# Turning x without its root: two transformer stacks on one core

## What is computed

```python
# first block, per layer
x = x + 0.5 * swiglu(rmsnorm(x, ffn1_norm), ffn1_w_in, ffn1_w_out)       # D_FF = 2816
x = x + hybrid_mixer(rmsnorm(x, mix_norm), w_in, ...)   # delta rule, stick-breaking attention, gates
x = x + 0.5 * swiglu(rmsnorm(x, ffn2_norm), ffn2_w_in, ffn2_w_out)
# second block, per layer
x = x + hybrid_mixer_2(rms_norm(x, mix_norm), ...)      # two attentions, gated mixing, w_out
x = x + memory_cross_attention(rms_norm(x, mem_x_norm), mem, ...)        # h @ mem_w_q, softmax, @ mem_w_o
x = x + conv_gated_ffn(rms_norm(x, ffn_norm), w_up, conv_w, conv_b, w_down)
# at the end
return rms_norm(x, final_norm)
# with
rmsnorm(x, g) = x * rsqrt(mean(x * x, over a row) + 1e-6) * g
swiglu(h, w_in, w_out) = (silu(h @ gate) * (h @ up)) @ w_out             # gate, up = halves of w_in
```

## Time and profile before

| | us |
|---|---|
| median of 3 runs | 2601.81 |
| lowest, highest | 2601.13, 2605.77 |
| profiled execution | 2607.15 |
| its span in the trace | 2605.3 |
| TensorE busy | 2448.4 (94%) |
| GpSimd busy | 1790.0 (69%) |
| ScalarE busy | 1115.8 (43%) |
| VectorE busy | 948.4 (36%) |

### The profile page before, as it was taken

One profiled execution on the slowest core, in us unless ns is written; L12 is line 12 of the kernel. 1 busy time (PEld: TensorE's weight loads), 2 busy tenths in 40 slices (PEclk: granted clock), 3 DMA queues, 4 the chain that ended last, 5 costly groups with the idle time before them and its releaser, 6 DMA issues.

```text
span 2605.3 us, 45928 instructions
## 1 busy us (share of the span) xinstructions
PE 2448.4 (94%) x17692; PEld 2292.1 (88%) x17692; DVE 948.4 (36%) x1554; ACT 1115.8 (43%) x1248; POOL 1790.0 (69%) x1372
## 2 busy tenths in 40 slices
PE   7999999998899999999999889999888999898998
PEld 7999888988899899888889889999788998787997
DVE  1114555322311211245543241112424564423564
ACT  4334434445333433444343634335454335454333
POOL 6998444455799789864445667996545997544996
PEclk9999999998999999999999899999899999899999
DMA  6554332323455455442233334564233555323553
GB/s 207 191 179 150 109 97 87 109 90 105 131 192 179 162 180 191 146 150 94 82 98 106 106 129 152 187 203 129 82 98 114 189 182 164 105 72 107 170 185 121
DMA packets 312052, 360.11 MB, mean 138 GB/s; under 512 B 18604, under 2 KB 290912, under 8 KB 311776
## 3 DMA queue, kind: packets, MB, share of 16 engines
q1 hardware_dynamic: 311904, 358.08, 42.4%
HBM read 357.00 MB, written 1.05 MB: 137 GB/s over the span
## 4 chain that ended last, share of the span: by engine, by line
POOL 43%; issue 26%; PE 25%; DVE 3%; ACT 2%; POOLq 0%; DVEq 0%; ACTq 0%
POOL sb_lo L458 43%; PE ps L482 21%; PE ps L911 1%; PE ps L887 1%; PE ps L799 1%; ACT sb_kT L1002 0%; ACT sb_sq L1328 0%; PE ps L524 0%; DVE sb_negmax L1802 0%; PE ps L960 0%; POOLq L453 0%; ACT sb_levels L1301 0%; PE ps L894 0%; DVE sb_kT L1745 0%; PE ps L869 0%
## 5 line engine op out<-in xcount | busy, mean ns | idle before, releaser
L458 POOL TENSOR_TENSOR sb_lo<-sb_raw,sb_hi 128x512 fp32r<-128x512 f32 x1368 | 1789.8, 1341 | 794.0 <-ACT sb_hi L991 791.8
L482 PE MATMUL ps<-sb_hT_h,sb_hi 128*128 128x256 f32 x3524 | 1026.6, 291 | 33.3 <-DVE sb_hT_l L1434 10.6
L482 PE MATMUL ps<-sb_hT_h,sb_lo 128*128 128x256 f32 x3524 | 1007.0, 286 | 0.0
L482 PE MATMUL ps<-sb_hT_l,sb_hi 128*128 128x256 f32 x3524 | 1006.6, 286 | 0.0
L991 ACT ACTIVATE sb_hi<-sb_raw 128x2048 fp32r<-128x2048 f32 x342 | 655.3, 1916 | 797.1 <-PE ps L482 792.3
L482 PEld LDWEIGHTS ps<-sb_hT_h,sb_hi 128*128 128x128 f32 x3524 | 684.5, 194 | 50.3 <-issue 31.3
L482 PEld LDWEIGHTS ps<-sb_hT_h,sb_lo 128*128 128x128 f32 x3524 | 685.3, 194 | 3.6 <-issue 1.4
L482 PEld LDWEIGHTS ps<-sb_hT_l,sb_hi 128*128 128x128 f32 x3524 | 684.6, 194 | 0.0
L482 PE MATMUL ps<-sb_hi,sb_o_h 128*128 128x512 f32 (+1 forms) x720 | 265.4, 369 | 9.9 <-DVE sb_o_l L1441 9.9
L482 PE MATMUL ps<-sb_hi,sb_o_l 128*128 128x512 f32 (+1 forms) x720 | 263.4, 366 | 0.0
L482 PE MATMUL ps<-sb_lo,sb_o_h 128*128 128x512 f32 (+1 forms) x720 | 262.7, 365 | 0.0
(11 more groups left out here) (320 smaller groups left out, 2811.0 us busy)
## 6 DMA issues: line engine op xcount, KB each, us to landing
sb_raw<-in_ffn_w_in SPq DMA_DIRECT2D x88, 1024.0 KB, 5.1
sb_raw<-in_w_in SPq DMA_DIRECT2D x78, 1024.0 KB, 5.2
sb_raw<-in_ffn_w_out SPq DMA_DIRECT2D x44, 1024.0 KB, 5.0
sb_raw<-in_ffn_w_up SPq DMA_DIRECT2D x44, 1024.0 KB, 5.1
sb_raw<-in_ffn_w_down SPq DMA_DIRECT2D x22, 1024.0 KB, 4.8
sb_raw<-in_w_out SPq DMA_DIRECT2D x16, 1024.0 KB, 5.1
sb_raw<-in_w_branch_a SPq DMA_DIRECT2D x8, 1024.0 KB, 5.1
sb_raw<-in_w_branch_b SPq DMA_DIRECT2D x8, 1024.0 KB, 5.1
```

The costliest lines, as they stand in the source:

```text
L458: ins = nc.gpsimd.tensor_tensor(lo[:, slot, c], raw[:, slot, c], hi[:, slot, c].bitcast(F32), ALU.subtract)
L482: ins = mm(dst, s, m, start=first and n == 0, stop=last and n == 3 * len(pairs) - 1)
```

## The change

1. **Networks, the memory's queries.** x is turned as it is (`turn`), without the root. The gain is applied as before in the high and low parts. The inverse root of each row is made meanwhile (`squares`, `diagonal`), put on the diagonal of a 128 x 256 tile, and one matmul with ones (`turn_row`) spreads it over all partitions; ScalarE copies it to `row` (`take_row`). VectorE multiplies the outputs by it in PSUM (`by_row`): gate and up of every chunk, and the memory's queries, which ScalarE no longer copies. Silu waits for `gate_scaled`. Mixers keep the old entry. The filler transposes ahead of the changed entries go.
2. **x comes in pieces.** Additions to x are in four pieces (strips of 256 columns after mixers, 512 columns of one row tile after networks and memory), each releasing `x_ready`. Groups of two block rows are turned as soon as their columns are there: three groups after mixers while the last units run, two groups inside the last unit after a network (only between layers of the first block) or memory.
3. **The first two units interleave** (`enter`): a part of the gate's block rows, the late transposes, the same part of the up unit, the row's matmul, the rest of the gate, the rest of up. On ScalarE the splits of the third and fourth unit stand before Silu of the first chunk as before, but between them the row is copied.
4. **Loads.** x in two tiles, the identity and ones come first, the rest of the constants after the first five units; the nine vectors of layer 0 go out on ScalarE's queue, those of layer 1 during the second network of layer 0. The first unit is split by quarters, on ScalarE and VectorE. The loop over the layers of the first block is written out.

```diff
+            def turn(g, bank):
+                for i in range(2):
+                    for t in range(ST):
+                        k = 2 * g + i
+                        ins = nc.tensor.transpose(ps[:, bank, i * S + t * P:i * S + (t + 1) * P], x[:, t, k * P:(k + 1) * P], ident)
+                ins.then_inc(tr_ready, 1)
+            def turn_row(e, bank):
+                pe.wait_ge(diag_ready, e + 1)
+                ins = mm(ps[:, bank, 0:S], cc("ones"), diag, start=True, stop=True)
+                ins.then_inc(row_turned, 1)
+            def enter(e, n, q, b, units, banks, row_bank, early, landed=True):
+                (u0, bank0), (u1, bank1) = units
+                split_at = 2 * early
+                feature_part(b, u0, bank0, q, 0, split_at, landed)
+                if early < 4:
+                    pe.wait_ge(x_ready, updates(n))
+                    for g in range(early, 4):
+                        turn(g, banks[g])
+                    feature_part(b, u1, bank1, q, 0, split_at)
+                    turn_row(e, row_bank)
+                    feature_part(b, u0, bank0, q, split_at, KB)
+                    feature_part(b, u1, bank1, q, split_at, KB)
+                else:
+                    turn_row(e, row_bank)
+                    feature_part(b, u1, bank1, q, 0, KB)
...
-                transposes(3 * l + 2)
-                ffn(2 * l + 1, b + (FFN_UNITS + MIX1_UNITS) // RING, 3 * l + 2, sil_ready, 2 * NCH * l + NCH)
+                enter(2 * l + 1, 3 * l + 2, 3 * l + 2, b2, ((0, AFTER_MIX_GATE), (1, 1)), TURN_BANKS, ROW_BANK, 3)
+                if l + 1 < DEPTH:
+                    columns(16 * V1_LOADS * (l + 2), 1, 2)
+                ffn(2 * l + 1, b2, sil_ready, 2 * NCH * l + NCH, 3 * l + 3 if l + 1 < DEPTH else None)
...
+            def enter(e, n, q, gain, banks, row_bank, early, next_split):
+                squares(n)
+                for g in range(early, 4):
+                    high_pair(q, g, gain, hT_h, banks[g])
+                diagonal()
+                next_split(0)
+                take_row(e, row_bank)
+                next_split(1)
...
+                def silu(j, bank=0):
+                    act.wait_ge(gate_scaled, F0 + j + 1)
+                    fn(sil[:], ps[:, bank, :], ACT.Silu).then_inc(sil_ready, 1)
-                split(b, 2)
-                split(b, 3)
-                silu(b, 0, None)
+                silu(0, bank_of_first)
...
-                def chunk(bb, ku, kd, j, parts=act_parts):
+                def chunk(bb, kg, ku, kd, j, parts=act_parts, bank=0):
+                    dve.wait_ge(unit_done, RING * bb + (kg + RING + 1))
+                    by_row(ps[:, bank, :], ps[:, bank, :]).then_inc(gate_scaled, 1)
                     dve.wait_ge(act_ready, F0 + j + 1)
+                    dve.wait_ge(unit_done, RING * bb + (ku + RING + 1))
+                    own.link(by_row(ps[:, 1, :], ps[:, 1, :]))
                     dve.wait_ge(sil_ready, F0 + j + 1)
-                    dve.wait_ge(unit_done, RING * bb + (ku + RING + 1))
                     tt(prod[:], sil[:], ps[:, 1, :], ALU.mult).then_inc(up_used, 1)
```

More of the change, by code:

```diff
@@ L199 @@
 WARM = 20
+PIECES = 4
 DELTA_WEIGHT = [2, 3, 2] + [1] * 10 + [1.3, 1, 1, 1, 1, 1, 1, 1.5, 2]
@@ L272, in build_program @@
         rstd = sb("rstd", [P, 8])
+        row = sb("row", [P, S])
         negmax = sb("negmax", [P, 2, 4])
@@ L373, in ffn @@
                 gate(0, 0), up(1, 0), gate(2, 1), up(3, 1), down(4, 0)
+                if between is not None:
+                    between()
                 with sp.Fori(1, NCH - 1) as j:
@@ new lines, in squares, with diagonal @@
+            def squares(n):
+                act.wait_ge(x_ready, updates(n))
+                for t in range(ST):
+                    ins = fn(junk[:, t, :], x[:, t, :], ACT.Square, accum_out=ss[:, t:t + 1])
+                own.link(ins)
+            def diagonal():
+                own.link(rsqrt(rstd[:, 0:ST], ss[:, 0:ST], 1.0 / D))
+                for t in range(ST):
+                    ins = fn(diag[:, t * P:(t + 1) * P], ident, ACT.Copy, scale=rstd[:, t:t + 1])
+                ins.then_inc(diag_ready, 1)
@@ L1400, in _ @@
                 mixer2(l, b)
-                high(q + 2, gain2(V2_ON), hT_h)
-                for r in range(13, 17):
+                high(q + 2, gain2(V2_ON), o_h)
+                for r in range(13, 15):
                     two_next(b, r)
@@ L1808, in memory @@
                 sig = lambda ins: ins.then_inc(me_dve, 1)
-                scaled(x, n)
-                low(q + 3, gain2(V2_MEMX), hT_h, hT_l)
+                low_pair(q + 3, 3, gain2(V2_MEMX), hT_h, hT_l, MEMORY_BANKS[3])
+                dve.wait_ge(row_ready, 2 * l + (2 * DEPTH + 1))
+                for m in range(2):
+                    dve.wait_ge(unit_done, RING * b + (17 + m + RING + 1))
+                    two = lambda v: v.rearrange("p (k n) -> p k n", n=S)
+                    sig(tt(qT[:, 2 * m:2 * m + 2, :], two(ps[:, 6 + m, :]), over(row[:], 2), ALU.mult))
                 for beta in range(ME_BATCHES):
```

449 lines of the change are left out of this document (284 added, 165 removed).

## The result

| kernel | us, median (lowest to highest, runs) | before, same chip | ratio, 95% interval |
|---|---|---|---|
| changed | 2572.16 (2570.52 to 2574.12, 4) | 2602.29 | 0.9879, 0.9867 to 0.9891 |
| changed, second time | 2571.30 (2569.56 to 2575.33, 4) | 2605.73 | 0.9875, 0.9860 to 0.9891 |

The change saves 30.1 us by the first pair of medians and 34.4 by the second. Predicted were 37.7, and 2564; the range 2550 to 2586 holds the time. By the two profiled executions it is 2607.15 - 2571.15 = 36.0, span 2569.2.

A forecast was written before the change was run, and what follows sets the result against it. TensorE is busy 94% of the span, idle between stages. Savings 4.2 + 7.1 + 9.4 + 9.9 + 8.8 + 1.3 - 3 = 37.7 take the profiled 2607.15 to 2569.5; the median, 5.3 lower, gives 2564, range 2550 to 2586.

The forecast's parts named there:

- the entries' chains: Step-by-step times at stage entries; mixer to network was to take 16.8 us against 18.9, saving 4.2 for two.
- The wait that it named: Entry from mixer to network: TensorE idle from 13.3 to 15.9 us until Silu has read the gate, about 2.6 us.
- The wait of 1.1 in three entries: Entries behind a network or memory: TensorE waits 1.1 us for the second transposed group's low part, behind VectorE's last addition.
- inside the networks: Turns of a network: two products by the row a chunk, 0.69 us each on VectorE, cost nothing under TensorE's 16.98.
- rival 3: Network turns: products by the row slow GpSimd until it bounds, 19.1 us a turn, 2694; chance 0.05 with other slowness.
- The price of the rival: Network turns: GpSimd becoming the bound decides from 1.2 us of added GpSimd time a turn.
- the clock: TensorE at half rate after idle stretches: 3 us charged for seven inner entries, bounds 0 to 17.
- Rival 1: Entries: unfilled gaps keep TensorE cold (17 us) and unfound waits add 8; about 15 saved, 2587; chance 0.20.
- the memory: Two entries from mixer to memory: scores start at 14.9 us against 19.6, saving 4.7 each, 9.4 for two.
- the start: Kernel start: x, identity and first unit load earlier, first two units done at 30.4 us against 39.2; 8.8 saved.
- the ends: Ends of five networks: last addition 512 wide, 0.69 us instead of 1.22; 1.3 saved for five, bounds 0 and 2.6.
- the right column of the table: Predicted savings by stretch of the whole kernel, without the 3 us charged for half rate; sum 40.7 us.

The follow-up runs named there:

- filler in the gaps: Changed kernel with 20 identity transposes on TensorE in each gap behind a mixer and 9 behind a network, first block; 2568.36 us (0.9859).
- the orders mended: Changed kernel, first block: Silu before unit 3's split, unit 2's split right behind the squares, vectors' copy behind chunk 0; 2568.56 us (0.9850).
- orders and PSUM: Changed kernel with the orders mended and VectorE's product of Silu and up written to PSUM in all six networks; 2566.44 us (0.9863).
- the version to beat both: Changed kernel: product in PSUM, unit 2's split behind squares, Silu first only behind a network, no wait for Silu behind a mixer; 2563.86 us (0.9844).

## Why the prediction was right or wrong

*Where it was right: the entries' chains.* Behind a mixer, counted from the last product (691.6), the prediction had low parts at 2.5, 36 matmuls at 5.4, the up unit's first part at 10.2, both units at 13.3 and Silu at 15.9. The trace has 2.4, 5.4, 10.2, 13.5 and 16.1. The wait that it named, split of unit 3, table load and Silu ahead of the next gate, is there: 2.70 and 2.82 us for 2.6. A second limit stands close behind it, unseen: VectorE's copy of the next vectors, which waits for TensorE's last transposes, is in front of the product by the row at 705.38, and with the split out of the way the gap there fell only to 2.10. The wait of 1.1 in three entries was 0.8 and twice 1.14. The table load again took 1.28 us, and Silu began right behind it (705.82, 707.12); the 2.7 us that the Trainium skill's page "ScalarE: Activation LUTs", section Terms, gives for it are not seen here.

*Right: inside the networks.* The products cost nothing there (16.98 a turn; the kernel without them is no faster in the four networks of the first block), and rival 3 fell by its own condition: one SBUF input, 699 ns in the mean of 132. The price of the rival was sound too: 1.3 us a turn is free. By the page "SBUF — State Buffer" of the Trainium skill, section "Who interferes with whom", an instruction with two SBUF inputs contends with GpSimd and one with at most one doesn't, outside the modes that use both ports, which a cast can enter. The prediction left that exception out. The traces agree with both halves: the same subtraction takes 1578 ns with two SBUF inputs and 691 with one, and the cast, with its one input in SBUF, does wait.

*Right in size: the clock.* 3 us were charged for the seven inner entries, near the low end of 0 to 17, without a row that gave the number. In both traces of the changed kernel two of the seven are at half rate, the ones behind a mixer; half of 3.11 and 3.13 us of work is an estimate of 3.1, and filler in the gaps brings 2.8 back. Rival 1 had this mechanism, and overpriced it. That the charge came out is a guess that held.

*Mis-sized: the memory, the start and the ends.* Against the right column of the table, the two stages of the memory are 1.9 us short. Of this 1.4 is one small instruction of the softmax, on a 128x4 tile: VectorE's L2003 takes 0.86 us beside GpSimd's subtractions, 0.17 before, where GpSimd had paused.
```profile
1962.35 0.17 DVE L1803 TENSOR_SCALAR sb_negmax<-sb_negmax 128x4 f32<-128x4 f32 x1
```
```profile
1939.57 0.86 DVE L2003 TENSOR_SCALAR sb_negmax<-sb_negmax 128x4 f32<-128x4 f32 x1
```
In the traces with the orders mended, with orders and PSUM, and of the version to beat both it takes under 0.2, and the memory's stages are 41.1 to 41.2 us instead of 41.8: GpSimd's place in time had changed, a term that the sum didn't have. From memory to network 2.4 us are missing by the first pair and 3.7 by the second. About 0.5 an entry is the chain itself, and at the end of each convolved network the product by the row lengthens VectorE's last chunk, so that TensorE has a gap of 0.64 ahead of the last down unit, 0.4 of it waiting, where the sum had no term; 0.3 an entry stays open. The 1.3 between the pairs is half rate that the first trace of before has at 2405.6 and its second hasn't: the prediction had counted it as a saving of the entry. The start brought 7.7 and 7.1 for 8.8: the copy of the vectors came at 10.55, as said (10.5), but part of the first two units ran at half rate. Behind the last network 0.8 is lost where 0.3 was to come: the first row tile of x is now complete one piece before the last, not half a unit, and its squares begin 0.64 us ahead of the last addition and no longer 1.46. GpSimd's 16.4 us in the convolved network passed the 16.2 that I had set.

*The rest is no merit of the change.* The mixers were to be 2.6 us longer, by the transposes moved into them, and were 3.2 and 3.8 shorter. They were at half rate for 17.0 and 10.2 us less; half of that, 8.5 and 5.1, is by estimate the most that this can have given back, so it covers the 5.8 by which the first pair passes its sum and not all of the 6.4 of the second. Why they keep the full rate longer isn't known. So profile against profile the changed stages fell 7 us short of their sum, the mixers ran 6 us ahead of theirs, and the two nearly cancelled, 36.0 for 37.7, which is luck. The forecast then carried this saving over to the median, 2601.81, which was 5.3 us below the profile it was counted against; with the 1.7 that the saving was short and 1.0 by which the median after lies above its profile, that makes the 8 us between 2564 and 2572.

*Not shown:* no run keeps the root and changes the rest, so how much is due to x turned without its root and how much to x in pieces isn't separated.

## What to carry to other kernels

When a change shortens the path to a stage, look at what the old path hid: here a table load and a split, which became the wait of TensorE, and the clock that this wait then cost. Where an engine waits for a buffer to be read, ask whether the next write goes to that buffer at all. And a helper engine that seldom pauses is a risk at 92% load: shift the work around it and an instruction of another engine may be held by it. No instruction whose source lay in PSUM, with at most one input in SBUF, was held in any of the traces.

## What the hardware showed

VectorE's cast of 128x512 from SBUF takes 0.43 us with GpSimd idle. Beside a subtraction it ends 0.28 us behind the end of that subtraction, in all 60 such places of the changed kernel's first trace: as a rule it takes 0.60 in the first block's networks and 1.06 in the convolved ones, at most 1.52, and 2.28 in the second trace. In 6 of the 12 traces of the changed kernel and its edits 19 casts and products with two SBUF inputs were held far longer, 7.4 to 15.6 us, beside six to thirteen subtractions in a row. Each of the 19 ended 0.3 to 0.6 us behind the last subtraction before a pause of GpSimd. No instruction with at most one SBUF input whose source is in PSUM was held. Most fell in the first three turns of a network, the latest in the seventh. What lets one instruction in between two subtractions and holds another isn't settled: four products a turn were never held while GpSimd worked up to 189 us without a pause.
